# Weight blocks split two ahead, their low parts moved to POOL, and norm sums added on VectorE

## The reference

```python
# first block, layer 0: short convolution and an RWKV-7 recurrence
z = rms_norm(x) * (1 + scale) + shift; z = z @ even_w_in
out = concat([conformer_conv(...) * silu(a_gate), rwkv7_mix(...) * silu(b_gate)]) @ even_w_out
# layer 1: sparse attention, each query keeps its 128 best keys by an index score
score = sum_h wi * relu(qi @ ki.T); top_val, top_idx = lax.top_k(score, 128)
out = (softmax(q @ k[top_idx].T) @ v[top_idx] * silu(g)) @ odd_w_out
x = rms_norm(x + gate * out, final_g)
# second block: mixer, product-key experts (128 x 128), a gated per-layer projection
h = x + concat([short_conv_mixer(...), pool_mixer(...)]) @ w_o
s = (rms_norm(h) @ w_q) against sub_keys; sv, si = top_k(s, 16)       # 8 heads, 2 halves
cand = sv[0][:, None] + sv[1][None, :]; top_s, pos = top_k(cand, 16)  # the expert and its softmax gate
h = h + sum_k gate_k * gelu(expert_u[e_k] @ xn) * expert_v[e_k]
h = h + sigmoid(rms_norm(h) @ w_ple_gate) * (p @ w_ple_proj)
return rms_norm(h)
```

## Time and profile before

| | |
|---|---|
| median of 3 runs | 3547.11 us (3545.16 to 3549.3) |
| the profiled execution | 3546.97 us, its span 3545.2 us |
| PE busy | 3196.4 us (90%) |
| DVE busy | 2242.9 us (63%) |
| ACT busy | 1236.1 us (35%) |
| POOL busy | 698.2 us (20%) |
| low parts in `wsp` | 121 on POOL, 2548 ns each; 186 on DVE, 1249 ns each |
| high parts in `wsp` | 307 on ACT, 1053 ns each |

### The profile page before, as it was taken

One profiled execution on the slowest core, in us unless ns is written; L12 is line 12 of the kernel. 1 busy time (PEld: TensorE's weight loads), 2 busy tenths in 40 slices (PEclk: granted clock), 3 DMA queues, 4 the chain that ended last, 5 costly groups with the idle time before them and its releaser, 6 DMA issues. The chain is left out here.

```text
span 3545.2 us, 40091 instructions
## 1 busy us (share of the span) xinstructions
PE 3196.4 (90%) x16316; PEld 2478.9 (70%) x16316; DVE 2242.9 (63%) x3522; ACT 1236.1 (35%) x1788; POOL 698.2 (20%) x464
## 2 busy tenths in 40 slices
PE   7788999997896899979897889969999999999997
PEld 4566767665674665757676768858888888888874
DVE  3689899644669755364787789846664444444434
ACT  3234443333322454222322246632223322222223
POOL 2344334321222111000002132212221111111100
PEclk9899999998898999989999989989999999999998
DMA  5211111234111110212123336655553333333330
GB/s 190 90 64 50 48 50 43 105 116 154 60 60 50 51 36 30 91 64 89 66 96 101 115 121 223 223 200 192 192 193 124 124 119 123 121 119 119 120 106 30
DMA packets 164952, 378.31 MB, mean 107 GB/s; under 512 B 10657, under 2 KB 77217, under 8 KB 164641
## 3 DMA queue, kind: packets, MB, share of 16 engines
q1 hardware_dynamic: 164768, 375.76, 31.1%
HBM read 318.04 MB, written 57.67 MB: 106 GB/s over the span
## 5 line engine op out<-in xcount | busy, mean ns | idle before, releaser
L626 PE MATMUL ps<-hT,wsp 128*128 128x512 f32 x2120 | 886.0, 418 | 146.2 <-POOL wsp L2241 51.3
L627 PE MATMUL ps<-hT,wsp 128*128 128x512 f32 x2120 | 849.6, 401 | 0.0
L628 PE MATMUL ps<-hT,wsp 128*128 128x512 f32 x2120 | 849.5, 401 | 0.0
L626 PEld LDWEIGHTS ps<-hT,wsp 128*128 128x128 f32 x2120 | 412.6, 195 | 271.3 <-issue 87.2
L628 PEld LDWEIGHTS ps<-hT,wsp 128*128 128x128 f32 x2120 | 412.1, 194 | 92.0
L627 PEld LDWEIGHTS ps<-hT,wsp 128*128 128x128 f32 x2120 | 413.8, 195 | 82.2 <-issue 4.1
L2241 POOL TENSOR_TENSOR wsp<-ring,wsp 128x1024 fp32r<-128x1024 f32 x121 | 307.8, 2548 | 746.5 <-ACT wsp L1092 746.5
L1092 ACT ACTIVATE wsp<-ring 128x1024 fp32r<-128x1024 f32 x307 | 317.4, 1053 | 145.7 <-PE ps L628 118.6
L2346 POOL TENSOR_TENSOR ex<-ex 128x512 fp32r<-128x512 f32 x128 | 175.4, 1384 | 930.6 <-ACT ex L1454 930.6
L2194 DVE TENSOR_TENSOR xT<-ps,xT 128x512 f32<-128x512 f32 x256 | 175.2, 688 | 288.8 <-PE ps L628 288.8
L627 PE MATMUL ps<-ex 128*128 128x512 f32 x832 | 324.4, 390 | 0.0
(11 more groups left out here) (366 smaller groups left out, 4650.9 us busy)
## 6 DMA issues: line engine op xcount, KB each, us to landing
ring<-in_eu SPq DMA_DIRECT2D x128, 512.0 KB, 3.3
ring<-in_ev SPq DMA_DIRECT2D x128, 512.0 KB, 3.5
gd<-oh SPq DMA_DIRECT2D x8, 4096.0 KB, 14.8
ex<-gd SPq DMA_DIRECT2D x32, 1024.0 KB, 6.5
ring<-in_ein SPq DMA_DIRECT2D x57, 512.0 KB, 3.2
ring<-in_oin SPq DMA_DIRECT2D x40, 512.0 KB, 3.2
ring<-in_ada SPq DMA_DIRECT2D x37, 512.0 KB, 3.2
ex<-zd SPq DMA_DIRECT2D x15, 1024.0 KB, 9.3
```

Of the source, the lines that this page charges most:

```text
L626: pe.matmul(out, W[0], R[0], start=first, stop=False)
L627: pe.matmul(out, W[0], R[1], start=False, stop=False)
L628: return pe.matmul(out, W[1], R[0], start=False, stop=last)
```

## The change

Three things change, and two small ones with them.

1. `walk` takes a function `split_to`, and after each piece that uses one unit n it calls it with n + 2. On ACT that is `hi_to`, on DVE and POOL `lo_to`, on SP the load that belongs to it, and on PE nothing. The calls for n + 1 that the pieces make themselves stay.
2. `on_pool` goes by the name of a unit's matrix. 76 units move from DVE to POOL: 16 of `win` and 8 of `wo` (mixer), 16 of `wq` (queries) and 36 of `eu` (the 32 of the key blocks and the last 4 of the hot loop). None moves the other way. `oout`, the odd units of `eout`, 8 units of the index stage, `pleg` and the expert loop stay with DVE.
3. Each tile is squared by ACT as soon as it is final, by a piece `square` that stands behind the piece that makes the tile. DVE adds the eight squares one after another into one tile, and PE sums that over partitions with a single matmul.
4. In the key blocks a piece `gates` (the subtraction on DVE, the exponential on ACT) stands ahead of `look`; before, it was part of `soft`.
5. On SP the wait for the stores to `gd` moves from `ex_begin` to `gload`, behind the loads and stores that stand between, and one wait for all `zd` stores in `ex_begin` goes; `gload` has its own for what it reads.

The core of the diff:

```diff
+    order += [("square", "n0", k) for k in range(KT)]
     order.append(("stat", "n0"))
...
         order.append(("ea", m, unit("eout", 2 * m)))
+        order.append(("square", "n1", m))
...
+            if half:
+                order += [("square", "n2", m), ("square", "nx", m)]
...
+        order.append(("gates", blk))
         for half in (1, 0):
             order.append(("look", blk, half))
             pre()
...
-        on_pool = set(range(16, 105)) | set(range(113, 121)) | set(range(129, 161))
-        on_pool |= {n for n, (name, u) in enumerate(UNITS) if name == "eu" and 32 <= u < 56}
+        def by_pool(name, u):
+
+            return (name in ("ein", "wq") or name == "eout" and u % 2 == 0 or name in ("win", "wo") or name == "oin" and not 16 <= u < 24
+                    or name == "eu" and u < NPRE * JC)
...
-        def walk(pieces):
+        one_unit = {"eb", "ea", "ki", "wi", "qi", "key", "value", "q", "gate", "oo", "pool_in", "bg", "cg", "vc", "wo", "wq",
+                    "pre", "ple"}
+
+        def walk(pieces, split_to):
+
             for name, *args in ORDER:
                 if name in pieces:
                     pieces[name](*args)
+                if name in one_unit:
+                    split_to(args[-1] + 2)
...
+            def total(tag, name):
+
+                out, free = (prep_b if tag == "n0" else all_b).open(("stat", tag), V, name, tag)
                 w.wait_ge(*free)
                 w.wait_ge(consts_in, 32)
-                for k in range(KT):
-                    w.wait_ge(scalar_done, A("sq", tag, k))
-                    pe.matmul(out, ones[:, :], tiles[k % len(tiles)], start=k == 0, stop=k == 7).then_inc(
-                        tensor_done, T.step("sum", tag, k))
+                w.wait_ge(vector_done, V("acc", tag, 7))
+                pe.matmul(out, ones[:, :], acc_of[tag], start=True, stop=True).then_inc(tensor_done, T.step("sum", tag))
...
+            def square(tag, k):
+
+                acc, tiles = acc_of[tag], squares[tag]
+                w.wait_ge(scalar_done, A("sq", tag, k))
+                if k:
+                    own()
+                    dve.tensor_tensor(acc, tiles[0] if k == 1 else acc, tiles[k % 4], ALU.add).then_inc(
+                        vector_done, V.step("acc", tag, k))
...
             def ex_begin():
                 all_done("ex")
+
+            def gload(c):
                 for s in st_out:
                     w.wait_ge(s, 64)
-                for s in z_out:
-                    w.wait_ge(s, 16 * 28)
-
-            def gload(c):
```

More of the change, by code:

```diff
@@ L275, in schedule @@
     order.append(("ogs", 1))
-    order += [("oo", half, m, unit("oout", 2 * m + half)) for half in range(2) for m in range(8)]
+    for half in range(2):
+        for m in range(8):
+            order.append(("oo", half, m, unit("oout", 2 * m + half)))
+            if half:
+                order += [("square", "n2", m), ("square", "nx", m)]
     order.append(("stat2",))
@@ L285, in schedule @@
     order.append(("yms",))
-    order += [("wo", m, unit("wo", m)) for m in range(8)]
+    for m in range(8):
+        order.append(("wo", m, unit("wo", m)))
+        order.append(("square", "nf", m))
     order.append(("stat", "nf"))
@@ L341, in schedule @@
     order.append(("norm", "np"))
-    order += [("ple", m, unit("pleg", m)) for m in range(8)]
+    for m in range(8):
+        order.append(("ple", m, unit("pleg", m)))
+        order.append(("square", "ng", m))
     order.append(("stat", "ng"))
@@ L1113, in ada @@
                     act.activation(rowT, dense.at["row", l, g], ACT.Copy).then_inc(scalar_done, A.step("row", l, g))
[L1115 to L1125, removed]
+            def square(tag, k):
+                if tag == "n0":
+                    w.wait_ge(x_in, 16)
+                else:
+                    w.wait_ge(vector_done, {"n1": V("ea", k), "n2": V("oo", 1, k), "nx": V("oo", 1, k), "nf": V("wo", k),
+                                            "np": V("v", NC - 1, k), "ng": V("ple", k)}[tag])
+                if k >= 4:
+                    w.wait_ge(vector_done, V("acc", tag, max(1, k - 4)))
+                g = {"scale": cols("final_g")[:, k:k + 1]} if tag == "nx" else {}
+                act.activation(squares[tag][k % 4], xT[:, k, :], ACT.Square, **g).then_inc(scalar_done, A.step("sq", tag, k))
             def root(tag, ap):
@@ L1355, in stat2 @@
             def stat2():
[L1356 to L1364, removed]
+                w.wait_ge(vector_done, V("both"))
+                act.activation(m2, m2, ACT.Sqrt).then_inc(scalar_done, A.step("rt", "n2"))
             def norm2():
@@ L1461, in v @@
                         hi_to(ns[-1] + 1 + dt // 2)
+                    if c == NC - 1:
+                        square("np", dt)
             def plep():
@@ L1478, in scalar_program @@
             start()
-            walk({"ada": ada, "stat": stat, "root": lambda tag: root(tag, msum), "norm": norm, "dense": dense_part,
+            walk({"ada": ada, "square": square, "root": lambda tag: root(tag, msum), "norm": norm, "dense": dense_part,
                   "lora": lora, "knr": knr,
@@ L1530, in turned, with mean, square @@
                         vector_done, V.step("gsc", l))
-            def mean(tag, out, psum, name="mean"):
-                dve.tensor_scalar(out, psum, 1.0 / D, 1e-6, ALU.mult, ALU.add).then_inc(vector_done, V.step(name, tag))
+            def mean(tag, out, psum):
+                dve.tensor_scalar(out, psum, 1.0 / D, 1e-6, ALU.mult, ALU.add).then_inc(vector_done, V.step("mean", tag))
+            def square(tag, k):
+                acc, tiles = acc_of[tag], squares[tag]
[4 more added lines that the diff above has]
+                        vector_done, V.step("acc", tag, k))
             def stat(tag):
-                w.wait_ge(tensor_done, T("sum", tag, 7))
+                w.wait_ge(tensor_done, T("sum", tag))
                 mean(tag, msum, (prep_b if tag == "n0" else all_b).at["stat", tag])
@@ L1975, in stat2 @@
             def stat2():
-                m2 = small[:, :, :].rearrange("p a n -> p (a n)")
                 dve.tensor_tensor(gsc[:, 0, :], cols("final_g"), cols("g_mix"), ALU.mult).then_inc(
                     vector_done, V.step())
[L1979 to L1982, removed]
+                w.wait_ge(tensor_done, T("sum", "nx"))
+                mean("n2", msum, all_b.at["stat", "n2"])
+                dve.tensor_scalar(m2, all_b.at["stat", "nx"], 1.0 / D, None, ALU.mult).then_inc(
+                    vector_done, V.step("mean", "nx"))
                 own()
                 dve.scalar_tensor_tensor(out=m2, in0=msum, scalar=1e-6, in1=m2, op0=ALU.mult, op1=ALU.add).then_inc(
-                    vector_done, V.step("mean", "n2"))
+                    vector_done, V.step("both"))
                 one_over("n2", m2)
@@ L2123, in sums, with gates @@
                     vector_done, V.step())
+            def gates(blk):
+                gt = ijg[:, 256:384].rearrange("p (h k) -> p h k", k=16)
+                w.wait_ge(tensor_done, T.was("ij", blk - 1))
+                dve.tensor_tensor(gt, tv, tv[:, :, 0:1].broadcast_to([128, 8, 16]), ALU.subtract).then_inc(
+                    vector_done, V.step("gt", blk))
             def soft(blk):
@@ L2195, in v @@
                         vector_done, V.step("v", c, dt))
+                    if c == NC - 1 and dt:
+                        square("np", dt - 1)
                     if dt % 2 == 0:
                         lo_to(ns[-1] + 1 + dt // 2)
+                if c == NC - 1:
+                    square("np", 7)
             def ple(m, n):
```

47 lines of the change are left out of this document (20 added, 27 removed).

## The result

The changed kernel takes 3464.8 us (median of 4 runs, 3461.77 to 3471.03) against 3546.14 before: a ratio of 0.977 (0.9755 to 0.9789), 81 us less where 98 were forecast. The profiled execution is the slowest of the four, 3471.03 us with a span of 3468.7, so the traces differ by 76.5 us. By milestones on PE (the start of the first matmul of a stage, or the end of the last one) the gain divides as follows; these are differences of two starts or ends in the two traces.

What follows compares the result with a forecast made beforehand. PE was taken as the bound, busy nine tenths of the span, with DVE bounding the index stage. Norm sums 26.6, key blocks 46 and other stalls 26.7 sum to 99.3 off 3546.97: 3448 us, eight-in-ten range 3425 to 3500.

Steps and rivals of the forecast that it cites:

- The term of 46: Key blocks: low parts on POOL and early gates let PE set the pace, 46 us saved, bounds 0 and 53.
- contended lookup: Rival, key blocks: DVE never gets ahead, so every block has a stall of 5.2 us; 3470 us, chance 0.17.
- DVE shut out: Rival, key blocks: each POOL low part stops DVE for 2.40 us, making DVE the bound; 3485 us, chance 0.12.
- Norm sums: All norms: one square, addition and matmul follow the last tile, shortening the wait for the mean; 26.6 us saved.
- near 3.7 each: Norms ng, nf and np: wait of 6.36 us falls to about 2.4, saving 11.1 us for the three.
- that low part goes to POOL: 7: End of the hot loop: DVE's 8.49 us wait for a high part goes; 7 us saved, bounds 3 to 8.49.
- The rule of the prediction: DVE instructions with two SBUF inputs and POOL ones reading SBUF exclude each other; DVE operation 2.79 us instead of 0.69.
- the loads of weights run three units ahead as before: SP's queue: only two waits move; weight loads keep their lead and end no stall in these stages.
- the 5 us of the forecast: Start of the expert loop: first gather can leave earlier as stores between go earlier; 5 us saved, bounds 0 to 6.0.
- two of the small terms: State half of `eo`: fewer waits, 4 us (0 to 8.7); start of `oo`: low part done earlier, 4.7 us (0 to 5.28).
- The mixer's term: Mixer: stall of 9.80 us goes, a later high part gives part back; 6 us saved, bounds 1 to 9.8.
- The slower rival: 76 units moved to POOL: POOL comes onto PE's path, each unit 1.19 us later; 3611 us, chance 0.06.

Runs made afterwards that it cites:

- e3: Changed kernel with low parts divided between DVE and POOL as before the change, splits still two ahead: 3535.4 us, ratio 0.9975 against the kernel before.
- e5: Changed kernel with the gates' subtraction and exponential back behind the lookup: 3487.51 us, ratio 0.9836 against the kernel before.
- e7: Changed kernel with the gate stage's two loads issued ahead of the last expert_v loads: 3459.57 us, ratio 0.9757 against the kernel before.
- e4: Changed kernel with splits one unit ahead in the hot loop only: 3458.77 us, ratio 0.9756 against the kernel before.
- e2: Changed kernel with each split added by the walk one unit ahead instead of two: 3467.04 us, ratio 0.9781 against the kernel before.
- e8: Changed kernel, splits one ahead from the key blocks' last unit on, expert loop's first gathers and gate stage's loads earlier: 3444.4 us, ratio 0.9713 against the kernel before.
- e6: Changed kernel with the expert loop's two first gathers behind the first and second of the last four expert_u units: 3459.22 us, ratio 0.9759 against the kernel before.
- e1: Kernel before with only the new norm sums (squares, DVE additions, one matmul): 3517.46 us, ratio 0.9923 against the kernel before.

## Why the prediction was right, and where it was not

The direction, the mechanism and most terms held; the forecast was 17 us too low. By the stretches of the two traces 22.8 us are missing (99.3 against 76.5): four terms behind the key blocks lack 25.3, and the others together gave 2.5 more than was said.

*Key blocks.* The term of 46 measured 48.2 (with the queries in it), and the reasoning held in its parts: PE sets the pace, each later block is 45.4 us, and what is late next is the eighth unit, 5.65 us in the first block (forecast 5) and 1.22 in the others (0.4; the lookup alone takes 5.61, not 4.8). The rivals of a contended lookup in each block and of DVE shut out did not come. `e3` and `e5` show that both causes named, the low parts in DVE's chain and the late gates, had to go.

*Norm sums.* Forecast 26.6, of which the pair, n1, nf and ng came within 0.6 each in the changed kernel. The price of the sum's matmul was read from a row of another form: 0.79 was forecast, the float32 matmul takes 1.10, most of the 1.28 us that DVE stands behind it. The step that failed is np, "near 3.7 each": the sum was ready sooner, but the projection's load was issued only at 3369, behind the last load of weights, and PE waited 4.02 us for it; its 32 matmuls then ran behind an idle stretch and took 15.68 us where they had taken 13.96. I had asked what the last tile waits for, and not what PE wants next. `e7` turned the loss of 2.6 into a gain of 3.4.

*The hot loop.* The step that failed is "that low part goes to POOL: 7", with nothing else in the loop. The wait of 8.49 did go, but the loop itself was counted as unchanged, though its units are split two ahead like all others. With that DVE waits 17.3 us for PE's buffer, which it had not done before. With one ahead the loop is 6.1 us shorter than before (`e4`), near the 7 that was forecast. The rule of the prediction, that DVE and POOL shut each other out, is at work in both kernels and does not make the difference.

*The start of the hot loop.* Forecast at nothing, it lost 2.8 us. In the changed kernel a high part stands on ACT ahead of the copies that DVE needs, 0.7 us, and POOL's low part of a unit two ahead (1985.62 to 1988.02) meets DVE's first conversion:

```profile
1986.29 2.28 DVE L2165 CAST px<-px 128x1024 bf16<-128x1024 f32 x1 [7.44 <-ACT px L1440]
```

The same conversion took 0.69 before, and in `e2` and `e8`, where no low part runs beside it and the stretch is back at 14.6. The prediction's rule spoke of operations with two inputs in SBUF; this one has one, and was held up all the same.

*The start of the expert loop.* The step that failed is "the loads of weights run three units ahead as before". The walk's call on SP is for n + 2 as well, so a load that waits for a split, which waits for PE, stood in front of the gather and ate the 5 us. `e2`, with one ahead, took 33.0 there, and `e6` shows the same by moving the gather. What the moved waits alone are worth was not run; `e1`, with the waits as before, took 34.0 there, so the 5 us of the forecast are not shown.

*The split two ahead.* In two of the small terms (4 and 4.7, measured 5.5 and 6.3) it did what was said, and `e1` and `e2`, with one ahead, have next to nothing of either (113.1 and 113.0 in the output of layer 0, 551.3 and 551.5 in attention): the wait of 5.28 us at the start of `oo` and the small waits for `wsp` in `eo` are gone, while the large wait for DVE's operations there stays (7.31 before, 7.78 after). The mixer's term (6, measured 4.9) came out near by luck. The step that failed is that the stall of 9.80 goes and only part of it comes back: PE stands 8.50 us for a low part, now POOL's and one unit later, and 3.5 of the 4.9 are there in `e1`, which splits as before. As a whole it gained nothing (`e2`), which the forecast, with its costs at zero, had missed.

*The index stage* stayed as it was, as the rows on DVE said. The slower rival, POOL on PE's path, showed in no stage.

## What to carry to other kernels

A second unit of lead is no free insurance: each queue that gets it (SP's included) has one more instruction that waits for a slot, in front of work that could go; give it where a stage stalls without it, not to all stages. Moving side work to an idle engine pays in stages whose other engine mostly does operations that the idle one does not shut out. Where they do shut each other out, count the waits behind it too: here the faster hot loop was the one in which DVE's instructions lost more time to POOL. When a step on the path becomes shorter, look at what its consumer needs besides, the next load above all.

## What the runs showed that I had not expected

The recurrence, whose instructions stand in the same order in all ten kernels profiled, took between 772 and 782 us from the first unit to its end: 781.9 before, 781.7 after, 772.0 in `e1`. That spread is as large as some of the gains here, so single traces were compared by stretches and kernels by medians of several runs. Both traces of the main comparison are near its upper end. What makes it was not tried.
